# Order of the two column halves in the middle term of a three-term fp32r product

## What is computed

```
h = h + 0.5 * swiglu_ffn(h, ffn1_g, ffn1_w_in, ffn1_w_out)
h = h + mixer(rmsnorm(h, mix_g))
h = h + 0.5 * swiglu_ffn(h, ffn2_g, ffn2_w_in, ffn2_w_out)

def swiglu_ffn(h, g, w_in, w_out):
    gate, up = jnp.split(rmsnorm(h, g) @ w_in, 2, axis=-1)
    return (jax.nn.silu(gate) * up) @ w_out
```

## Time and profile before

| | us |
|---|---|
| median of 3 runs | 2575.29 (2573.64 to 2575.78) |
| the profiled execution | 2575.13 |
| its span, first to last instruction | 2573.2 |
| PE matmul busy | 2534.7 (99%) |
| PE weight load busy | 2463.8 (96%) |
| DVE busy | 1057.4 (41%) |
| ACT busy | 694.6 (27%) |
| POOL busy | 344.2 (13%) |

### The profile page before, as it was taken

One profiled execution on the slowest core, in us unless ns is written; L12 is line 12 of the kernel. 1 busy time (PEld: TensorE's weight loads), 2 busy tenths in 40 slices (PEclk: granted clock), 3 DMA queues, 4 the chain that ended last, 5 costly groups with the idle time before them and its releaser, 6 DMA issues.

```text
span 2573.2 us, 44082 instructions
## 1 busy us (share of the span) xinstructions
PE 2534.7 (99%) x18791; PEld 2463.8 (96%) x18791; DVE 1057.4 (41%) x1556; ACT 694.6 (27%) x990; POOL 344.2 (13%) x273
## 2 busy tenths in 40 slices
PE   9999999999999999999999999999999999999998
PEld 8999999989898979999999999999998789999998
DVE  4332334553635465332334333323335654332333
ACT  4221222222213222221222232212223542221221
POOL 0100113120101012100113221100121022100112
PEclk9999999999999999999999999999999999999999
DMA  5232233222222122232332432322233422232231
GB/s 150 82 102 62 85 93 89 75 78 74 87 67 90 54 66 83 82 102 63 89 94 72 140 104 85 96 82 74 86 86 107 116 78 82 82 101 63 82 96 48
DMA packets 393653, 221.71 MB, mean 86 GB/s; under 512 B 8032, under 2 KB 385984, under 8 KB 393520
## 3 DMA queue, kind: packets, MB, share of 16 engines
q1 hardware_dynamic: 388688, 205.13, 27.6%
q0 software_dynamic: 4640, 14.58, 1.7%
q10 hardware_dynamic: 192, 0.04, 0.0%
HBM read 206.01 MB, written 13.71 MB: 85 GB/s over the span
## 4 chain that ended last, share of the span: by engine, by line
PE 96%; DVE 2%; ACT 1%; issue 0%; DMA 0%; SPq 0%; POOL 0%; ACTq 0%; DVEq 0%; POOLq 0%
PE ps L1508 87%; PE ps L1887 1%; PE ps L1691 1%; PE ps L1677 1%; PE ps L1679 1%; PE ps L1678 1%; DVE wl L589 1%; PE ps L1915 1%; PE ps L1939 1%; PE ps L1711 0%; DVE xl L899 0%; PE ps L1792 0%; PE ps L1670 0%; DVE h L944 0%; DMA xtok<-in_x_sample 0%
## 5 line engine op out<-in xcount | busy, mean ns | idle before, releaser
L589 DVE TENSOR_TENSOR wl<-raw,wh 128x1024 fp32r<-128x1024 f32 (+3 forms) x352 | 450.8, 1281 | 1280.0 <-ACT wh L584 1280.0
L1508 PE MATMUL ps<-xh,wl 128*128 128x288 f32 x4000 | 861.7, 297 | 5.2 <-DVE xl L899 2.7
L1508 PE MATMUL ps<-xh,wh 128*128 128x288 f32 x4000 | 853.4, 295 | 0.0
L1508 PE MATMUL ps<-xl,wh 128*128 128x288 f32 x4000 | 853.1, 295 | 0.0
L584 ACT CAST wh<-raw 128x1024 fp32r<-128x1024 f32 (+3 forms) x352 | 375.9, 1068 | 1158.9 <-PE ps L1508 1158.0
L1508 PEld LDWEIGHTS ps<-xh,wl 128*128 128x128 f32 x4000 | 643.0, 189 | 11.5 <-issue 3.9
L1508 PEld LDWEIGHTS ps<-xh,wh 128*128 128x128 f32 x4000 | 643.3, 189 | 0.0
L1508 PEld LDWEIGHTS ps<-xl,wh 128*128 128x128 f32 x4000 | 643.3, 189 | 0.0
L1508 PE MATMUL ps<-actl,wh 128*128 128x288 f32 x1408 | 301.1, 295 | 0.0
L1508 PE MATMUL ps<-acth,wl 128*128 128x288 f32 x1408 | 301.0, 295 | 0.0
L1405 POOL TENSOR_TENSOR rsilu<-silu,rstd 128x576 f32<-128x576 f32 x88 | 125.9, 1430 | 1294.9 <-ACT silu L637 1294.9
(11 more groups left out here) (248 smaller groups left out, 1663.4 us busy)
## 6 DMA issues: line engine op xcount, KB each, us to landing
raw<-in_ffn_w_in SPq DMA_DIRECT2D x176, 512.0 KB, 3.8
raw<-in_ffn_w_out SPq DMA_DIRECT2D x32, 768.0 KB, 4.8
raw<-in_ret_w_in SPq DMA_DIRECT2D x48, 512.0 KB, 3.8
raw<-in_ffn_w_out SPq DMA_DIRECT2D x32, 640.0 KB, 4.3
raw<-in_ret_w_out SPq DMA_DIRECT2D x32, 256.0 KB, 2.7
raw<-in_fox_w_kvf SPq DMA_DIRECT2D x16, 512.0 KB, 4.1
raw<-in_fox_w_q SPq DMA_DIRECT2D x8, 512.0 KB, 4.8
bias<-cum_scratch SPq DMA_DIRECT2D x16, 256.0 KB, 3.4
```

Source lines behind the costliest of these rows:

```text
L589: nc.vector.tensor_tensor(wl[:, s % SPLIT, 0:kt, :], raw[:, s, 0:kt, :], wh[:, s % SPLIT, 0:kt, :].bitcast(F32), ALU.subtract).then_inc(lo ...
L1508: mm = nc.tensor.matmul(out[:, a:z], w, x[:, a:z], start=start and n == 0, stop=stop and n == len(terms) - 1)
```

## The change

In the second of the three terms (`n` is 1) the columns 288 to 575 are now issued before the columns 0 to 287. Terms one and three keep their order. It holds for every caller of `product`.

```diff
             def product(out, terms, start, stop):
 
                 for n, (w, x) in enumerate(terms):
-                    for a, z in CUTS:
+                    for a, z in CUTS if n % 2 == 0 else CUTS[::-1]:
                         mm = nc.tensor.matmul(out[:, a:z], w, x[:, a:z],
                                               start=start and n == 0, stop=stop and n == len(terms) - 1)
                 return mm
```

## The result

The changed kernel takes 2586.07 us (2583.35 to 2588.54, 5 runs) beside 2575.06 (2573.38 to 2575.78, 5 runs): a ratio of 1.0046, 95% interval 1.0033 to 1.0059. It is slower by 11 us, clear of noise. The profiled execution is its quickest, 2583.35 us with a span of 2581.4, so the spans differ by 8.2.

What follows compares the result with a forecast made beforehand. The prediction took TensorE's spacing of matmul starts as the bound. A span of 2573.2 us plus 1.9 outside it made 2575.1; with every step taken as 0, the forecast was 2575 us, range 2538 to 2598.

Steps and rivals of the forecast that it cites:

- What bounds the kernel: The rate at which TensorE starts one product after the other; PE busy over 99%, longest wait sums 4.2 us.
- Step (a): Two neighbours writing one bank, 5776 times: at most 0.5 ns each, 3 us; taken as 0.
- Step (b): Order in which halves of the moving tile are read: new order taken to average today's 132.2 ns, change 0.
- The bounds: Read order, all matmuls: at 130.0 ns 37 us less, at 133.2 18 more, two of six pausing 37 more.
- The slower rival: Second FFN input parts lose 12 us, output products 6: 2593; 2612 with two pauses in six everywhere. Chance 0.32.
- The quicker rival: Stretches at 133.2 ns fall to 130.0, 26 us less: 2549; 2538 with output products too. Chance 0.32.
- The start of a stretch: Pause present in stretches that follow a wait, absent in those behind an unbroken run of output products: 133.2 against 130.0 ns.
- the rule that was weighed: Gap depends on columns alone: 122.5 ns here, so the change would have no effect; the prediction didn't count it as proof.

Runs made afterwards that it cites:

- gap_before_second: Kernel before, with PE waiting in front of each second FFN input part until all earlier sums are taken: 2606.98 us, 1.0130.
- banks_reversed: Kernel before, with the middle term writing the second bank first but reading in the old order: 2574.47 us, 0.9997.
- mixed: Kernel before, with the middle term reversed everywhere but in second FFN input parts and products on acth, ogh or foxh: 2582.09 us, 1.0033.
- weights_shift64: Kernel before, with wh and wl alone 64 bytes higher in SBUF and all tiles behind them 512 bytes higher: 2581.95 us, 1.0029.
- mixed_handover: As mixed, but with the old order in the last four units of each first FFN input part: 2568.88 us, 0.9975 of the kernel before.
- shift64: Kernel before, with all tiles of the stage regions (acth, actl, ogh, foxh and neighbours) 64 bytes higher in SBUF: 2592.56 us, 1.0067.
- nudge_second: Kernel before, plus one unread matmul of 64 to 256 columns behind the first four units of each second FFN input part: 2583.34 us, 1.0037.
- mixed_nudged: As mixed, with second FFN input parts reversed too and an unread 64-column matmul behind the first four units of each: 2580.89 us, 1.0026 of the kernel before.
- after_nudge_second: Changed kernel, plus the same extra matmuls as nudge_second in the second FFN input parts: 2582.43 us, 1.0027 of the kernel before.

## Why the prediction was wrong

**What bounds the kernel** was right: the spacing of TensorE's products and nothing else; no wait, DMA or other engine took part in any run but gap_before_second, which puts waits in. (The busy share is 98.5% before and after, 2534.7 of 2573.2 us, and not over 99%.)

**Step (a), the same bank twice, taken as 0**, was right: banks_reversed has it alone and is at 0.9997. The bound from the 512-column products, 0.5 ns at most, held.

**Step (b), the read order, taken as 0**, is the step that failed. The bounds were sound: -37, +18, +37, and +11 came out. The choice between them was not. I argued that some other rhythm would come and would have the average of today. The first half was so, though 133.3 ns can be held in the new order too; the second was a guess with no row behind it, and three stretches that move by +3.3, +1.2 and -1.5 ns have no reason to add up to nothing. What the rows did say was that 3840 matmuls stood in the rhythm without a pause, and a stretch that has none can only lose. That is +13 us, against which the slow stretches could give back at most 26 and gave back 12 by the estimate above, 7 of it in stretches that are shown.

**The slower rival** was this mechanism. It had the second input parts at +12 us (13 measured) and the output products at +6 (6 measured). It took the slow stretches as unchanged, and there the reversed order gained these 12 us that only the quicker rival had foreseen in kind. With both terms it would have said 2582. It got 0.24 where it should have been the forecast.

**The quicker rival** named the right place, the first parts, but its rhythm of 130.0 appears in no stretch of the changed order in any run; 131.7 does.

**The start of a stretch** was read rightly from the table (slow behind a wait, quick behind running output products), and then not used. It wasn't only a description: which rhythm the second parts have is handed to them, and a change that never touches them can cost 13 us (mixed).

On the rule that was weighed: N/2.4 + 2.5, which the Trainium skill, page "TensorE: Matmul & The Clock Gate", section "Back-to-back issue gap", gives for an isolated matmul, is not this kernel's spacing at any of its values, nor does its zero effect hold. The Trainium skill, page "TensorE: Matmul & The Clock Gate", section "Step-by-step: what each phase is for", says too that loading the next tile's weights does not steal SBUF read bandwidth from the running matmul. weights_shift64 speaks against taking that for all operands: with wh and wl moved by 64 bytes and nothing else moved to a grid of 512, input products went from 130.0 and 133.2 ns to 132.2, and output products from 132.1 to 133.1. These are fp32r operands; no run here moves any others.

## What to carry to other kernels

Where one engine is busy 99% of the time, read its spacing stretch by stretch before a change, and where one form of instruction has several spacings, treat the quickest as something the change can lose. Reordering equal products, or moving a tile by 64 bytes, was worth from -0.25% (mixed_handover) to +0.67% (shift64) in this kernel of fp32r products back to back; it is no matter of which order is better in itself, so measure it with what stands ahead of it, and again when anything there changes. A difference of this size between two versions need not come from the lines that were edited.

## What was not expected of the hardware

- The same matmul (128x288, fp32r, full clock) has spacings of 130.0, 131.0, 131.7, 132.2 and 133.3 ns, each kept for hundreds of matmuls. Which one holds depended on the order of reads, on the place of the moving operand to the weights' (0 or 64 bytes to a grid of 128), and, at one and the same order and place, on what ran before.
- One extra matmul of 64 to 256 columns moved a stretch of 768 from 130.1 to 133.2 ns (nudge_second); one of 64 columns moved such a stretch of the changed order from 131.7 to 133.3 (mixed_nudged) and from 133.3 to 131.7 (after_nudge_second).
- Two neighbours that write the same bank have no price here (banks_reversed, 0.9997).
- Behind a wait of 3.1 us the granted clock was at the 1.2 GHz level in four of four cases, and matmuls took 442 ns in place of 293 (gap_before_second).
